# Closing the two banks of a product one after the other, with a token for each

## What is computed

```python
# first block
mod = silu(c) @ w_ada + b_ada; shift, scale, gate = split(mod)
h = rms_norm(x, g_pre) * (1 + scale) + shift
q_mla, kv_a, z_mla, qkv_dil, z_dil, gl_mla, gl_dil = split(h @ w_in)
a = mla_branch(q_mla, kv_a, positions, g_kv, w_kv_b) * silu(z_mla)
bb = dilated_branch(qkv_dil, positions) * silu(z_dil)
merged = sigmoid(gl_mla) * (a @ w_mla_proj) + sigmoid(gl_dil) * (bb @ w_dil_proj)
x = x + gate * rms_norm(merged @ w_o, g_post)
# second block, two layers
y = sparse_attention(x, w_in_a) @ w_out_a        # layer 0
y = stick_breaking(x, k_b, v_b, w_q_b) @ w_out_b # layer 1
x = layer_norm(ALPHA * x + y, ln_g[i], ln_b[i])
x = x + (p[i] @ w_ple[i]) * sigmoid(x @ w_ple_gate[i])
```

## Time and profile before

| | |
|---|---|
| median of the runs | 2448.31 us |
| lowest and highest | 2445.65 and 2450.62 us |
| the profiled execution | 2449.69 us |
| its span, first to last instruction | 2448.3 us |
| TensorE (PE) busy | 97% |
| DVE, ACT, POOL busy | 61%, 46%, 5% |
| TensorE pauses for wlo | 17.1 us in 14 pauses |

### The profile page before, as it was taken

How to read it: one execution, slowest core, us unless ns; L and a number is a source line. 1 busy time by engine, 2 the same in 40 slices (tenths; PEclk the granted TensorE clock), 3 DMA queues, 4 the chain that set the end, 5 groups by cost and what they waited for, 6 DMA issues and landing times.

```text
span 2448.3 us, 28030 instructions
## 1 busy us (share of the span) xinstructions
PE 2371.4 (97%) x11164; PEld 1963.0 (80%) x11164; DVE 1484.0 (61%) x2072; ACT 1123.8 (46%) x1472; POOL 117.2 (5%) x136
## 2 busy tenths in 40 slices
PE   7899999989999999999999999999999999999998
PEld 4567888878888898788888888888778878888777
DVE  6887565444445544677665676566655455465664
ACT  4233444534445454444344445554445555455443
POOL 1000000000000000000000100000100011010010
PEclk9999999989999999999999999999999999999999
DMA  9886544435553455888555644445665445545564
GB/s 357 320 317 245 161 137 146 159 111 188 183 190 116 149 183 200 308 289 280 178 182 180 202 148 171 166 161 180 220 201 189 173 172 172 175 162 180 184 221 172
DMA packets 135845, 478.94 MB, mean 196 GB/s; under 512 B 15793, under 2 KB 16049, under 8 KB 134689
## 3 DMA queue, kind: packets, MB, share of 16 engines
q1 hardware_dynamic: 130688, 458.42, 54.0%
q0 software_dynamic: 3728, 17.76, 2.0%
q10 hardware_dynamic: 1298, 0.97, 0.1%
HBM read 470.80 MB, written 6.29 MB: 195 GB/s over the span
## 4 chain that ended last, share of the span: by engine, by line
PE 80%; DVE 6%; ACT 3%; issue 1%; DMA 1%; DVEq 0%; ACTq 0%
PE G L470 24%; PE G L472 24%; PE G L471 24%; PE A L545 4%; DVE wlo L380 2%; PE A L794 1%; PE A L818 1%; ACT whi L378 1%; ACT dil L500 1%; PE A L994 1%; DMA raw<-in_weights 1%; DVE dil L1741 0%; PE A L1469 0%; DVE CP L1747 0%; PE A L960 0%
## 5 line engine op out<-in xcount | busy, mean ns | idle before, releaser
L380 DVE TENSOR_TENSOR wlo<-raw,whi 128x1024 fp32r<-128x1024 f32 (+2 forms) x774 | 926.6, 1201 | 729.1 <-ACT whi L378 726.7
L378 ACT ACTIVATE whi<-raw 128x1024 fp32r<-128x1024 f32 (+2 forms) x774 | 792.1, 1025 | 843.7 <-PE G L472 732.6
L470 PE MATMUL G<-whi,XH 128*128 128x512 f32 (+3 forms) x2804 | 1088.3, 388 | 20.5 <-DVE wlo L380 17.1
L472 PE MATMUL G<-whi,XL 128*128 128x512 f32 (+3 forms) x2804 | 1068.4, 381 | 0.0
L471 PE MATMUL G<-wlo,XH 128*128 128x512 f32 (+3 forms) x2804 | 1067.8, 381 | 0.0
L470 PEld LDWEIGHTS G<-whi,XH 128*128 128x128 f32 x2804 | 528.1, 188 | 122.0 <-DVE wlo L380 20.9
L472 PEld LDWEIGHTS G<-whi,XL 128*128 128x128 f32 x2804 | 527.3, 188 | 95.5
L471 PEld LDWEIGHTS G<-wlo,XH 128*128 128x128 f32 x2804 | 528.2, 188 | 90.1 <-issue 0.5
L330 DVE CUSTOM_DVE_ANT_0 raw<-raw,dil 128x1024 f32<-128x1024 f32 x64 | 84.9, 1340 | 10.5 <-DMA raw<-in_weights 10.5
L470 PE MATMUL A<-whi,XH 128*128 128x512 f32 x164 | 70.1, 427 | 6.6 <-DVE XL L646 3.4
L500 ACT ACTIVATE nat<-G 128x512 f32<-128x512 f32 (+4 forms) x102 | 51.2, 557 | 46.5 <-PE G L472 44.9
(11 more groups left out here) (198 smaller groups left out, 1599.3 us busy)
## 6 DMA issues: line engine op xcount, KB each, us to landing
raw<-in_weights SPq DMA_DIRECT2D x792, 512.0 KB, 4.2
raw<-in_weights SPq DMA_DIRECT2D x80, 384.0 KB, 3.0
raw<-in_weights SPq DMA_DIRECT2D x16, 288.0 KB, 2.8
spill<-nat POOLq DMA_DIRECT2D x8, 512.0 KB, 4.1
CP<-spill POOLq DMA_DIRECT2D x8, 512.0 KB, 4.7
raw<-in_weights SPq DMA_DIRECT2D x8, 336.0 KB, 3.1
FT<-in_xT SPq DMA_DIRECT2D x4, 512.0 KB, 5.8
Xn<-in_x POOLq DMA_DIRECT2D x1, 2048.0 KB, 11.8
```

Source lines behind the costliest of these rows:

```text
L378: th = AC.mark(nc.scalar.activation(h[:, 0:2 * cols], r[:, 0:2 * cols], ACT.Copy))
L380: tl = VE.mark(nc.vector.tensor_tensor(l[:, 0:2 * cols], r[:, 0:2 * cols], h[:, 0:2 * cols].bitcast(F32), ALU.subtract))
L470: nc.tensor.matmul(o, h, wh, start=(k == start), stop=False)
L472: ins = nc.tensor.matmul(o, l, wh, start=False, stop=(k == nkt - 1))
```

## The change

In a product's last group the order of the four (kk, hf) parts becomes (0, 0), (1, 0), (0, 1), (1, 1) in place of (0, 0), (0, 1), (1, 0), (1, 1): the first half of the rows is finished after six of the twelve matmuls. The sixth raises the semaphore too, and each bank carries a token of its own, `done`; readers of a bank wait for that in place of the product's token. The planner's clock is advanced by half a group before each of the two marks. Everything else that waits for a product (buffers of the split, `mm_done`, `x_read`) keeps the last matmul's token.

```diff
@@ class Bank
         self.t = t
+        self.done = None
         self.free = []
@@ gemm_slot
-            for kk in range(2):
+            last = k0 + 2 == nkt
+            us = 3.45 if s in whole else 12 * (cols + 32) / 2400.0
+            for kk, hf in ((0, 0), (1, 0), (0, 1), (1, 1)) if last else ((0, 0), (0, 1), (1, 0), (1, 1)):
                 k = k0 + kk
                 PE.wait(full_ready[k] if s in whole else ready[k])
-                for hf in range(2):
-                    o = pair[hf].t[:, 0:cols]
...
+                o = pair[hf].t[:, 0:cols]
...
                     ins = nc.tensor.matmul(o, l, wh, start=False, stop=(k == nkt - 1))
-            PE.busy(3.45 if s in whole else 12 * (cols + 32) / 2400.0)
-            t = PE.mark(ins)
+                if last and (kk, hf) == (1, 0):
+                    PE.busy(us / 2)
+                    pair[0].done = PE.mark(ins)
+            PE.busy(us / 2 if last else us)
+            t = pair[1].done = PE.mark(ins)
+            if not last:
+                pair[0].done = t
             mm_done[s] = t
@@ to_nat
-                    VE.wait(t, free.get(key))
+                    VE.wait(pair[hf].done, free.get(key))
...
-                tk = act_copy(buf[:, hf, 0:cols], pair[hf].t[:, 0:cols], [t, free.get(key)], func, **kw)
+                tk = act_copy(buf[:, hf, 0:cols], pair[hf].t[:, 0:cols], [pair[hf].done, free.get(key)], func, **kw)
@@ partial sums of the opening
-                        tk = act_copy(dst, src, [t, part_tok[e][hf]])
+                        tk = act_copy(dst, src, [pair[hf].done, part_tok[e][hf]])
                     else:
-                        VE.wait(t, part_tok[e][hf])
+                        VE.wait(pair[hf].done, part_tok[e][hf])
@@ product with w_o
-                ts = act_copy(sq[:, :], pair[hf].t[:, :], [t, free.get("sq")], ACT.Square,
+                ts = act_copy(sq[:, :], pair[hf].t[:, :], [pair[hf].done, free.get("sq")], ACT.Square,
@@ layer_norm
-                    VE.wait(t)
+                    VE.wait(pair[hf].done)
```

More of the change, by code:

```diff
@@ L455, in gemm_slot @@
                     pump()
-            for kk in range(2):
+            last = k0 + 2 == nkt
+            us = 3.45 if s in whole else 12 * (cols + 32) / 2400.0
+            for kk, hf in ((0, 0), (1, 0), (0, 1), (1, 1)) if last else ((0, 0), (0, 1), (1, 0), (1, 1)):
                 k = k0 + kk
                 PE.wait(full_ready[k] if s in whole else ready[k])
-                for hf in range(2):
-                    o = pair[hf].t[:, 0:cols]
[L461 to L465, removed]
+                o = pair[hf].t[:, 0:cols]
+                if s in whole:
+                    ins = nc.tensor.matmul(o, full[:, k, hf * 128:(hf + 1) * 128],
+                                           in_raw(n)[:, kk * cols:(kk + 1) * cols],
+                                           start=(k == start), stop=(k == nkt - 1))
+                else:
                     h = xh[:, k, hf * 128:(hf + 1) * 128]
@@ L1208, in gate_chunk @@
             for hf in range(2):
-                tk = act_copy(GL[g][:, hf, 512 * c:512 * c + 512], pair[hf].t[:, :], [t, *gl_free], ACT.Sigmoid)
+                tk = act_copy(GL[g][:, hf, 512 * c:512 * c + 512], pair[hf].t[:, :], [pair[hf].done, *gl_free], ACT.Sigmoid)
                 pair[hf].free = [tk]
@@ L1281, in first_and_second_block @@
                 dst = GL[0][:, hf, 512 * c:512 * c + 512]
-                VE.wait(t, *gl_t[0][c])
+                VE.wait(pair[hf].done, *gl_t[0][c])
                 tk = VE.mark(nc.vector.tensor_tensor(dst, pair[hf].t[:, :], dst, ALU.mult))
@@ L1330, in first_and_second_block @@
                 d1 = GL[1][:, hf, 512 * c:512 * c + 512]
-                VE.wait(t, *gl_t[1][c])
+                VE.wait(pair[hf].done, *gl_t[1][c])
                 tk = VE.mark(nc.vector.tensor_tensor(d1, pair[hf].t[:, :], d1, ALU.mult))
```

## The result

The changed kernel takes 2434.94 us (median of four executions, 2433.05 to 2436.12); the kernel before 2446.98 (four executions, 2445.18 to 2450.62). The ratio is 0.9948, with an interval of 0.9936 to 0.9961: 12.0 us less, where 6.8 was forecast.

A forecast was written before the change was run, and what follows sets the result against it. TensorE, busy 97% of the span, was taken as the bound, so only its pauses and the end could shrink. Eight terms summed to 6.8 us, giving 2441.5 us from the median of 2448.31, range 2437.5 to 2449.0.

The forecast's parts named there:

- end: Behind the last matmul: the first half's copy and two DVE operations run before the product ends, minus 1.35 us.
- gate: First embedding gate, TensorE's 3.56 us pause: the eviction chain shortens by DVE's idle time before it, minus 0.95 us.
- w_o: Norm after w_o, TensorE's 1.32 us pause: one of two ACT squares runs earlier, minus 0.70 us.
- MLA quad: End of the second MLA quad, 1.27 us pause: half of two ACT copies goes ahead, minus 0.54 us.
- layer norms: Two layer norms: DVE's chain shortens, but embedding products cover most; the 0.39 us pause goes twice, 0.8 us.
- opening's last operand rows: Opening, 1.83 us pause for the scaled operand: one of DVE's two bank additions goes ahead, minus 0.65 us.
- indexer's chunk: Indexer's second query chunk, 1.14 us pause: POOL's rotary multiplies and DVE's wlo end earlier, minus 0.80 us.
- last query chunk: Last query chunk of the first mixer, 1.50 us pause: POOL and wlo end earlier, 1.00 us gained.
- places 2 and 6: First embedding gate and the opening's scaled operand: shorter eviction chains gain 0.95 and 0.65 us.
- second rival: Transposes of eight moved products stand ahead of their rotary operands and stop TensorE: 6.1 us slower, 2454.4; chance 0.10.
- The first: Layer norms, opening, both query chunks: DVE's queue, POOL or weight DMA holds pauses; only 3.5 us gained, 2444.8; chance 0.30.
- The third: Where a transposed tile's copy precedes the product's in ACT's queue, the early token is worthless; stays 2448.3; chance 0.08.

The follow-up runs named there:

- e1: The changed kernel's early tokens and matmul order, but the plan counts the first bank's token as late as the product's, keeping the order of before: 2433.92 us, ratio 0.9945.
- e2: The changed kernel's program and plan, but each reader of a first bank really waits for the product's last matmul: 2450.30 us, ratio 1.0010 to the kernel before.
- e12: The changed kernel, but in the last stick-breaking attention chunk the plan counts the first bank's token as late as the product's: 2429.71 us, ratio 0.9923 to before.
- e11: e1 without the early token in the opening and at the third product of the first embedding gate: 2439.69 us, ratio 0.9963 to the kernel before.
- e7: The kernel before, with the new matmul order and the early token only in the opening's partial sums: 2446.09 us, ratio 0.9992.
- e4: The kernel before with only the matmul order of a product's last group changed; all readers wait for the last matmul: 2447.36 us, ratio 0.9999.
- e5: The kernel before, with the new matmul order and the early token only at the third product of the first embedding gate: 2445.03 us, ratio 0.9992.
- e9: The kernel before, with the new matmul order and the early token only at the first two merge gates: 2447.86 us, ratio 0.9998.

## Why the prediction was right in its parts and wrong in its sum

**The eight terms held.** Forecast and measured, after against before: end 1.35 and 1.33; gate 0.95 and 1.06; w_o 0.70 and 0.72; MLA quad 0.54 and 0.49; layer norms 0.80 and 0.79 (the two pauses, 0.39 and 0.40, are gone); opening's last operand rows 0.65 and 0.59; indexer's chunk 0.80 and 1.14 (its pause is gone; 0.97 of it by the token, as in e1, the rest by the order); last query chunk 1.00 and 1.01. Together 6.8 and 7.1. The method, an eviction chain with idle time ahead of it becomes shorter by a half, was right at each place. (The caps of the terms add to 7.7 us, 1.35 + 0.95 + 0.70 + 0.54 + 0.80 + 0.74 + 1.14 + 1.50, not to the 8.2 that the prediction gives; with them the bound on the gain would have been nearer 9.7 than 10.5, and the miss larger.)

**The step that failed is the price of a pause.** The prediction began with the premise that the change "can only shorten TensorE's pauses and the stretch behind the last matmul"; so each term counted the pause, and the matmuls behind it were put at nothing. At places 2 and 6 TensorE's clock had fallen behind the pause, and the rows for that stood in the trace of before: 0.50 and 0.51 in the stretches shown above. Over all traces: behind the gate's pause of 3.56 us the clock was halved in seven of eight kernels, behind 2.50 in none of five; behind the opening's 1.83 in seven of seven, behind 1.24 in none of eight. The matched rows put this at 1.6 us in the opening and 1.5 to 1.6 at the gate. Place 4 belongs here too: behind the MLA quad's 1.27 the clock is halved from 490 on in six of seven traces (not in e2), behind 0.78 in none of eight, though no run has the token at this place alone. These are the matmuls behind that pause in before and in after:

```profile
490.10:493.40 3.30, 3.30 (x16) 0.50 0.02 5
```

```profile
486.20:489.50 3.30, 3.30 (x23) 1.00 0.10 37
```

That gives 1.6 us by 494, but the stretches at half clock that follow lie elsewhere then, and by 515 the matmuls of after are only 0.6 us ahead of those of before (0.6 to 4.5 in the eight traces, 0 to 3.2 in the seven). Nor does every stretch at half clock cost: five of the fifteen traces, among them four with the token, have one near 85 in the opening, which takes 0.8 us, and by 94 all of it has come back, because the pause that follows, for DVE's additions, is that much shorter. The Trainium skill (TensorE: Matmul & The Clock Gate, "Part 1: The HAM clock gate") says that the array's clock is passed at one of two rates, set by TensorE's recent activity; the rows agree: stretches read 0.50 or 1.00, and values between only where the change falls inside the stretch.

**The opening was read from one row.** The pause for XL near 63 (1.54, now 1.05) and that for wlo near 234 (1.08, now 0.64) have the same cause as the one that was priced; 0.9 us was missing.

**The order counted as nothing.** Six pairs of transposes in the second unit do stand after the second group, 0.97 us behind the last rotary operation, and no pause: the second rival didn't come about. But the plan moved steps at places that the prediction didn't look at. Two gains: a pause of 0.93 at 255.85 is gone, and one of 1.51 at 1422.3 is 0.75. Three small pauses of 0.14 are new. In the last chunk a new pause of 1.38, less 0.6 of an earlier one, and the half clock behind it cost 2.3 in the trace, which e12 undid.

**The sum again.** The pause in brackets is counted from the modelled end of the matmul before it, so it can be too short: at each layer norm TensorE's first group starts 0.63 us sooner in e1, where the pause of before read 0.39, and at 1499.3, 1551.7 and 1604.0 the token brings 0.24 us each where no row of before shows a pause. So the table compares the starts of TensorE's rows, which stand in the same order but for the moved transposes. After is 14.4 us ahead at the end, the difference of the two spans (2448.3 and 2433.9):

| where | us gained |
|---|---|
| the eight terms | 7.1 |
| the other two pauses of the opening | 0.9 |
| clock at places 2 and 6 | 3.3 |
| clock between 490 and 515 | 0.6 |
| layer norms, beyond their pauses | 1.3 |
| moved steps, 236 to 280 and 1358 to 1640, net, the three starts among them | 2.0 |
| last chunk | -2.3 |
| near 983 | 2.4 |
| first 84 us, without the pause for XL | -1.0 |

The last two rows aren't shown to be the change's (the seven traces without a token in the opening differ by 2.5 us in the first 60 us). Without them it is 12.9, for 12.0 between the medians. e11 is 8.0 less than before, for 4.9 of terms; the same starts give 0.5 more at the layer norms, 0.7 at the three places near 1500 to 1604, 0.7 between 490 and 515, and 1.3 near 983 if that is the tokens': 3.2 for the 3.1 that the terms leave.

**The rivals.** The first (at places 5 to 8 another cause stands behind the pause) fell: all four shrank as computed. The third (the token does not reach the evictions) fell with ACT's first copy at 2427.59, ahead of the last matmul.

## What to carry to other kernels

Price a pause of TensorE with the granted clock of the microseconds behind it: where that reads 0.5, shortening the pause can be worth its own length and up to 1.6 us more, unless a wait behind it takes the time back, and an edit that sets two small pauses close together can pay that price anew. Where a program is laid out by due times, split a changed token into the token and its due time and measure the two apart: here the token was worth 15 us, and the order that it induced cost 2.3 us in one chunk and gave some 2 us elsewhere. A wait that only a forced drain causes is worth looking for as soon as the chain behind it is short: moving that drain gave another 3 us.

## What the runs showed of the hardware

- The same pause doesn't always bring the clock down: behind 3.56 us it stayed at 1.00 in one of eight traces (e7), and e4, whose time is that of before, has a half-clock stretch at 984 and none at 510, where before has the reverse. Near 984 five of fifteen traces have one (e1, e4, e5, e7, e9), with the token or without. This may be part of why executions of one kernel differ by up to 8 us; one trace of each kernel can't show it.
- A 512 KB weight took 4.4 us to land in some executions and 3.3 in others over the same 18 us ahead of POOL's loads, in programs of the same order, while it took the same 3.3 to 3.4 between 300 and 900 us in before, e4 and after.
- Twelve matmuls that alternate between two banks and twelve in two runs of six take the same time (ratio 0.9999; six in one bank took 1.36 us in after, 2427.16 to 2428.52).
